# First block of a two-block layer: modulation products shared with TensorE, and moved past other work

## The reference, cut to what matters

```python
ada = c @ w_ada[layer] + b_ada[layer]                    # 1024 -> 6144
shift1, scale1, gate1, shift2, scale2, gate2 = split(ada, 6)
h = rms_norm(x, g_norm1) * (1 + scale1) + shift1
z = h @ w_in                                             # 3524 wide
q, k, ik = rms_norm(zq), rms_norm(zk), rms_norm(zik)     # per head
y_attn = dsa_attention(q, k, zv, ziq, ik, ziw) @ w_up_attn
y_pool = pool_mixer(zp, w_pool_grp, s_pool) @ w_up_pool
mixed = (g_attn * y_attn + g_pool * y_pool) @ w_out
x = x + gate1 * mixed
h2 = rms_norm(x, g_norm2) * (1 + scale2) + shift2
x = x + gate2 * peer_ffn(h2, ...)                        # 16384 experts
```

## Time and profile before

| | |
|---|---|
| median of 3 runs | 1739.95 us (1735.2, 1740.91, 1739.95) |
| profiled execution, own time | 1738.6 us, span 1736.8 us |
| mean granted clock of TensorE | 0.970 |
| PE busy | 1597.0 us (92%) |
| DVE busy | 1170.0 us (67%) |
| POOL busy | 1153.6 us (66%) |
| ACT busy | 867.8 us (50%) |

### The profile page before, as it was taken

How to read it: one execution, slowest core, us unless ns; L and a number is a source line. 1 busy time by engine, 2 the same in 40 slices (tenths; PEclk the granted TensorE clock), 3 DMA queues, 4 the chain that set the end, 5 groups by cost and what they waited for, 6 DMA issues and landing times.

```text
span 1736.8 us, 27719 instructions
## 1 busy us (share of the span) xinstructions
PE 1597.0 (92%) x9959; PEld 1398.7 (81%) x9959; DVE 1170.0 (67%) x1695; ACT 867.8 (50%) x1475; POOL 1153.6 (66%) x468
## 2 busy tenths in 40 slices
PE   1788977999999999999999999899978988899999
PEld 1665536999999999978888888889757756789987
DVE  6564546899937777768888888652995276268760
ACT  1443204555566666645555555559634455354452
POOL 0662005689986666668888888759974821668886
PEclk9899889999999999999999999999989899999999
DMA  7645255455454444445555555546544610445554
GB/s 266 222 150 193 100 218 188 157 181 176 161 184 143 137 143 137 146 141 192 192 194 191 192 193 194 164 159 195 179 136 130 198 61 13 145 146 184 182 183 143
DMA packets 79271, 286.94 MB, mean 165 GB/s; under 512 B 8785, under 2 KB 9297, under 8 KB 79058
## 3 DMA queue, kind: packets, MB, share of 16 engines
q1 hardware_dynamic: 78464, 283.51, 49.1%
q10 hardware_dynamic: 722, 2.27, 0.4%
HBM read 284.70 MB, written 1.05 MB: 165 GB/s over the span
## 4 chain that ended last, share of the span: by engine, by line
PE 77%; DVE 11%; POOL 4%; ACT 3%; issue 3%; DMA 2%; ACTq 0%; SPq 0%; POOLq 0%; DVEq 0%
PE PS L340 22%; PE PS L341 21%; PE PS L342 21%; POOL low L1921 4%; PE PS L338 3%; DVE region L1743 2%; DMA ring<-in_stream 2%; PE PS L719 2%; PE PS L461 1%; PE PS L718 1%; DVE region L1460 1%; PE PS L783 1%; PE PS L551 1%; ACT region L979 1%; DVE region L1747 1%
## 5 line engine op out<-in xcount | busy, mean ns | idle before, releaser
L1921 POOL TENSOR_TENSOR low<-ring,high 128x1024 fp32r<-128x1024 f32 x464 | 1153.4, 2498 | 572.5 <-ACT high L914 572.2
L914 ACT ACTIVATE high<-ring 128x1024 fp32r<-128x1024 f32 x464 | 488.2, 1058 | 438.3 <-PE PS L342 412.8
L340 PE MATMUL PS<-hTh,high 128*128 128x256 f32 (+1 forms) x1728 | 494.1, 286 | 6.1 <-POOL low L1921 4.6
L341 PE MATMUL PS<-hTl,high 128*128 128x256 f32 (+1 forms) x1728 | 489.6, 283 | 0.0
L342 PE MATMUL PS<-hTh,low 128*128 128x256 f32 (+1 forms) x1728 | 489.0, 283 | 0.0
L340 PE MATMUL PS<-high,hTh 128*128 128x512 f32 x960 | 381.7, 398 | 18.2 <-POOL low L1921 14.1
L341 PE MATMUL PS<-low,hTh 128*128 128x512 f32 x960 | 377.8, 394 | 0.0
L342 PE MATMUL PS<-high,hTl 128*128 128x512 f32 x960 | 377.3, 393 | 0.0
L340 PEld LDWEIGHTS PS<-hTh,high 128*128 128x128 f32 (+1 forms) x1728 | 322.9, 187 | 7.9 <-POOL low L1921 3.9
L1691 DVE TENSOR_TENSOR hTl<-region,hTh 128x256 fp32r<-128x256 f32 x128 | 289.2, 2260 | 58.7 <-ACT hTh L1146 58.7
L341 PEld LDWEIGHTS PS<-hTl,high 128*128 128x128 f32 (+1 forms) x1728 | 323.0, 187 | 0.1
(11 more groups left out here) (282 smaller groups left out, 1634.2 us busy)
## 6 DMA issues: line engine op xcount, KB each, us to landing
ring<-in_stream SPq DMA_DIRECT2D x536, 512.0 KB, 3.3
X<-in_x SPq DMA_DIRECT2D x1, 1024.0 KB, 4.9
region<-in_band ACTq DMA_DIRECT2D x1, 1024.0 KB
result<-X SPq DMA_DIRECT2D x4, 256.0 KB, 2.0
region<-in_skeys ACTq DMA_DIRECT2D x1, 512.0 KB
region<-in_consts ACTq DMA_DIRECT2D x1, 352.0 KB, 3.6
region<-in_wpool ACTq DMA_DIRECT2D x1, 256.0 KB
cols<-in_cols SPq DMA_DIRECT2D x1, 228.0 KB, 5.0
```

Of the source, the lines that this page charges most:

```text
L340: pe.matmul(out_, sh, mh, start=start, stop=False, **kw)
L341: pe.matmul(out_, sh, ml, start=False, stop=False, **kw)
L914: act.activation(high[:, b % RING, :], ring[:, b % RING, :], ACT.Copy).then_inc(rounded[b % RING], 1)
L1921: pool.tensor_tensor(low[:, b % RING, :], ring[:, b % RING, :], high[:, b % RING, :].bitcast(F32), ALU.subtract).then_inc(left[b % RING], 1)
```

## The change

- Start: each of `ada` 0 to 3 is shared out. TensorE takes quarters 0 and 2 (`ADA_ON_PE`): two float32 matmuls for each, whose stationary operand is one column of `c` and whose moving operand is 512 columns of weights; the result is one row of PSUM. ACT copies that row to SBUF, and TensorE's sums take it in by one more matmul per 128 outputs (a stationary operand of one partition), 16 passes in place of 8. DVE does quarters 1 and 3. TensorE does the products of block j before the sums of block j-1.
- The decay constants move on DVE from behind `ada(0)` to behind the attention, and their exponential on ACT to just before the attention.
- Queries and keys: per token tile, two `tensor_tensor` of 128 columns (broadcast inputs) in place of four `tensor_scalar` of 64; the copy of 256 columns goes, and TensorE transposes those two chunks from `Z`.
- `ada(9)` and `ada(4)` on DVE move into the attention, one quarter behind each of the eight units. The stream's order becomes `up_pool`/`ada8`, `ada9`, `ada4`, `up_attn`.
- The sums of `ada` 6 to 9 on TensorE move behind the transposes of the mixed sum; the wait for `ada_kept` moves from before `out0` to behind it.
- The mixed sum: `up_attn` finishes its last two quarters bank by bank, into banks 4 to 7, and signals each bank. DVE mixes a bank as it comes; the transposes of the first four chunks need three banks mixed, the others all four.

```diff
-    for name in [f"in{i}" for i in range(Z1B)] + ["up_pool", "up_attn", "ada4", "out0", "out1", "pq0", "pq1"]:
+    for name in [f"in{i}" for i in range(Z1B)] + ["up_pool", "ada9", "ada4", "up_attn", "out0", "out1", "pq0", "pq1"]:
...
+        ADA_ON_PE = (0, 2)
...
             def transposes(tag, src, ready, n_ready, chunk=None, first_half=None):
-                pe.wait_ge(sem(ready), n_ready)
+                pe.wait_ge(sem(ready), first_half or n_ready)
                 for c in range(KC):
+                    if first_half and c == KC // 2:
+                        pe.wait_ge(sem(ready), n_ready)
...
-                        last = pe.matmul(PS[:, 7, 4 * j + q:4 * j + q + 1], src[:, q * P:(q + 1) * P],
-                                         ones[:, 0:1], start=True, stop=True)
+                        dst = PS[:, 7, 4 * j + q:4 * j + q + 1]
+                        last = pe.matmul(dst, src[:, q * P:(q + 1) * P], ones[:, 0:1], start=True, stop=(j >= 4))
+                        if j < 4:
+                            last = pe.matmul(dst, ada_row[0:1, j, q * P:(q + 1) * P], ones[0:1, 0:1],
+                                             start=False, stop=True)
...
+            def ada_products(j):
+                for q in ADA_ON_PE:
+                    wait_loaded(pe, f"ada{j}", q)
+                    for c in range(2):
+                        last = pe.matmul(PS[0:1, 5 + j % 2, :], col("cT", 2 * q + c), slot(f"ada{j}", q)[:, c, :],
+                                         start=(q == ADA_ON_PE[0] and c == 0), stop=(q == ADA_ON_PE[-1] and c == 1))
+                    if q != ADA_ON_PE[-1]:
+                        free_slot(f"ada{j}", q, last)
+                free_slot(f"ada{j}", ADA_ON_PE[-1], last)
...
-            for j in range(4):
-                wait_used(pe, f"ada{j}")
-                ada(j)
+            for j in range(5):
+                if j < 4:
+                    if j >= 2:
+                        pe.wait_ge(sem("ada_row_kept"), j - 1)
+                    ada_products(j)
+                if j:
+                    wait_used(pe, f"ada{j - 1}")
+                    pe.wait_ge(sem("ada_row_kept"), j)
+                    ada(j - 1)
...
-            for j in (6, 7, 8):
+            attention("a1")
+
+            pe.wait_ge(sem("attn1_kept"), 2)
+            token_major("up_attn", OT1, lambda t, o: 4 + 2 * t + o, per=1, inner=D, bank_done="up_done")
+            transposes("m1", M1, "m1_ready", 4, first_half=3)
+            for j in (6, 7, 8, 9):
                 wait_used(pe, f"ada{j}")
                 ada(j)
-            attention("a1")
-
-            pe.wait_ge(sem("attn1_kept"), 2)
-            token_major("up_attn", OT1, lambda t, o: 2 * t + o, per=1, inner=D)
-            wait_used(pe, "ada9")
-            ada(9)
-            transposes("m1", M1, "m1_ready", 1)
             pe.wait_ge(sem("turned_kept"), kept_by("m1", KC))
-            pe.wait_ge(sem("ada_kept"), 2)
...
             token_major("out0", MT1, lambda t, o: 4 + 2 * t)
+            pe.wait_ge(sem("ada_kept"), 2)
...
+            for j in range(4):
+                wait_used(act, f"ada{j}", ADA_ON_PE[-1])
+                act.activation(ada_row[0:1, j, :], PS[0:1, 5 + j % 2, :], ACT.Copy).then_inc(sem("ada_row_kept"), 1)
...
+                    if tag == "a1" and u < n:
+                        ada((9, 4)[u // QUARTERS], [u % QUARTERS])
...
-                for dup in range(2):
-                    dve.tensor_scalar(N1[:, t, 512 + dup * HD:576 + dup * HD], Z[:, t, K1:K1 + HD],
-                                      st1[:, 2, r0 + 8:r0 + 9], None, ALU.mult)
-                    dve.tensor_scalar(N1[:, t, 896 + dup * HD:960 + dup * HD], Z[:, t, IK1:IK1 + HD],
-                                      st1[:, 2, r0 + 9:r0 + 10], None, ALU.mult)
-                link(dve.tensor_copy(N1[:, t, 640:896], Z[:, t, IQ1:IQ1 + 256]))
+                for w, (o, src) in enumerate(((512, K1), (896, IK1))):
+                    ins = dve.tensor_tensor(N1[:, t, o:o + P].rearrange("p (e d) -> p e d", e=2),
+                                            bc(Z[:, t, src:src + HD], 1, 2),
+                                            st1[:, 2, r0 + 8 + w:r0 + 9 + w].unsqueeze(1).broadcast_to([P, 2, HD]),
+                                            ALU.mult)
+                link(ins)
...
             for t in range(T):
                 for half in range(2):
+                    if t and half:
+                        wait_used(dve, "up_attn")
+                    else:
+                        dve.wait_ge(sem("up_done"), 2 * t + half + 1)
                     o = half * NB
-                    res = PS[:, 2 * t + half, :]
+                    res = PS[:, 4 + 2 * t + half, :]
                     link(dve.tensor_tensor(res, res, Z[:, t, G1 + o:G1 + o + NB], ALU.mult))
-                    link(dve.tensor_tensor(M1[:, t, o:o + NB], res, y_pool[:, t, o:o + NB], ALU.add))
-            dve.memset(m8[:, :], 0.0).then_inc(sem("m1_ready"), 1)
+                    dve.tensor_tensor(M1[:, t, o:o + NB], res, y_pool[:, t, o:o + NB],
+                                      ALU.add).then_inc(sem("m1_ready"), 1)
```

More of the change, by code:

```diff
@@ L81 @@
 NCOL = _at
-PAIRED = {"in1": "ada6", "in6": "ada7", "up_pool": "ada8", "up_attn": "ada9", "out0": "ada5", "out1": "ada10",
+PAIRED = {"in1": "ada6", "in6": "ada7", "up_pool": "ada8", "out0": "ada5", "out1": "ada10",
           "pq1": "ada11"}
@@ L215, in build_program @@
         late_acc = take(ADA_B - 4, NB)
+        ada_row = late_acc[0:1, 0:4, :]
         y_pool = XN1
@@ L612, in _ @@
                 z1(i)
-            transposes("qk1", N1, "qk1_normed", 1)
+            transposes("qk1", N1, "qk1_normed", 1, lambda t, c: (Z if c in (5, 6) else N1)[:, t, c * P:(c + 1) * P])
             z1(3)
@@ L1074, in _ @@
             keep_turned("m1", MT1)
+            act.wait_ge(sem("ada_summed"), 8)
+            act.activation(adaT[:, 24:40], PS[:, 7, 24:40], ACT.Copy).then_inc(sem("ada_copied"), 1)
             for i in range(2):
@@ L1445, in bc, with ada @@
                 return v.broadcast_to(shape)
-            def ada(j):
+            def ada(j, part=range(QUARTERS)):
                 if j in (2, 3):
                     dve.wait_ge(sem("ada_summed"), j - 1)
-                for q in range(QUARTERS):
+                qs = [q for q in range(QUARTERS) if j >= 4 or q not in ADA_ON_PE]
+                for n, q in enumerate(qs):
+                    if q not in part:
+                        continue
                     wait_loaded(dve, f"ada{j}", q)
                     w = slot(f"ada{j}", q)
-                    if q:
-                        wait_used(dve, f"ada{j}", q - 1)
+                    if n:
+                        wait_used(dve, f"ada{j}", qs[n - 1])
                     for c in range(2):
-                        if q == c == 0:
-                            ins = dve.tensor_scalar(ada_acc(j), w[:, 0, :], col("cT", 0), None, ALU.mult)
+                        if n == c == 0:
+                            ins = dve.tensor_scalar(ada_acc(j), w[:, 0, :], col("cT", 2 * q), None, ALU.mult)
                         else:
@@ L1473, in _ @@
             ada(0)
-            dve.wait_ge(sem("lam_exp"), 1)
-            link(dve.tensor_scalar(s[3], s[1], 2.0, None, ALU.add))
-            link(dve.reciprocal(s[4], s[3]))
-            link(dve.tensor_tensor(s[5], s[1], s[4], ALU.mult))
-            link(dve.tensor_tensor(s[6], s[5], s[5], ALU.mult))
-            link(dve.tensor_scalar(s[7], s[6], 1.0 / 15, 1.0 / 13, ALU.mult, ALU.add))
-            for k in (11, 9, 7, 5, 3, 1):
-                link(dve.tensor_tensor(s[7], s[7], s[6], ALU.mult))
-                link(dve.tensor_scalar(s[7], s[7], 1.0 / k, None, ALU.add))
-            link(dve.tensor_tensor(s[7], s[7], s[5], ALU.mult))
-            link(dve.tensor_scalar(s[7], s[7], 8.0, None, ALU.mult))
-            link(dve.tensor_scalar(s[2], s[2], 0.0, 4.0, ALU.max, ALU.mult))
-            link(dve.tensor_tensor(s[7], s[7], s[2], ALU.add))
-            dve.tensor_scalar(s[6], s[7], -2.0, None, ALU.mult).then_inc(sem("decay_ready"), 1)
             for j in range(1, 4):
@@ L1568, in _ @@
             dve.wait_ge(sem("ada_copied"), 1)
-            link(dve.tensor_tensor(adaT[:, 24:36], adaT[:, 24:36], bada[:, 24:36], ALU.add))
-            dve.wait_ge(sem("ada_summed"), 8)
-            dve.tensor_tensor(adaT[:, 36:40], PS[:, 7, 36:40], bada[:, 36:40], ALU.add).then_inc(sem("ada_kept"), 1)
+            dve.tensor_tensor(adaT[:, 24:40], adaT[:, 24:40], bada[:, 24:40], ALU.add).then_inc(sem("ada_kept"), 1)
             dve.wait_ge(sem("ada_kept"), 2)
```

27 lines of the change are left out of this document (18 added, 9 removed).

## The result

The changed kernel took 1718.58 us (median of 1725.23, 1718.58 and 1715.51), against 1739.95. The ratio is 0.9893, 95% interval [0.9857, 0.993].

The account below looks back on a forecast made before the run. PE, busy 92% of the span, was taken as the bound, with time gained only where it waits or runs slowly. Terms -3.8 - 0.9 + 3.0 - 6.7 + 2.2 = -6.2 us gave 1733.7 us, range 1727 to 1746.

Parts of the forecast that it names:

- From `up_attn` to `out0`: Stretch from `up_attn` to `out0`: 24.9 us in place of 31.6, 6.7 us gained.
- low start of `up_attn`: At `up_attn`: products start at the low clock, adding 2.5 us to 14.4 us.
- Attention: In the attention: sums ahead go, 3.75 us earlier, but DVE's quarters lengthen it; 3.0 us lost, bounds 0 and 5.
- Start: Modulation blocks 0 to 3: DVE leaves the path, last sums end at 38.8 against 42.6 us, 3.8 us gained.
- rival 2: At the start: one-column products never lift the clock, PE becomes the bound; 1745.5 us, chance 0.16.
- rival 1: At the start: clock flips, up in products and down in sums, so nothing is gained; 1738 us, chance 0.20.
- the ring: At the start: loop of filling and using weight slots, 6.1 to 6.5 us per block, level with PE's 6.2.
- Queries and keys: Query and key normalisation: new `tensor_tensor` still wait for POOL; 0.9 us gained, bounds 0.5 and 8.
- the bound of 8 us for no waits: At queries and keys: upper bound if DVE never waits for POOL, chain ending at 91 us.
- `out0` starts low: At `out0`: the sums ahead make the clock fall, so it starts low; 2.2 us lost, bounds 0 and 3.
- theory A: Experiments' theory: gain lies where the change works, mostly between `up_attn` and `out0`; what lies behind is carried one for one.
- B: Experiments' other theory: a good part of the gain is how low-clock stretches fall, in the block and behind it.

Follow-up runs that it names:

- e1: The changed kernel run again with no edit: median 1718.39 us, ratio 0.9888 to the kernel before.
- e4: The changed kernel with the keys scaled by ScalarE, VectorE left only the two 512-column `tensor_tensor`: median 1713.96 us, ratio 0.9864.
- e7: The changed kernel with all four banks mixed at once after the last product, not bank by bank: median 1729.65 us, ratio 0.9952.
- e9: The changed kernel with the 32 sums of `ada` 6 to 9 behind `out1` instead of ahead of `out0`: median 1718.39 us, ratio 0.9895.
- e10: The changed kernel with keys scaled on ScalarE and the sums of `ada` 6 to 9 behind `out1`: median 1706.19 us, ratio 0.984.
- e3: The changed kernel with the start undone (modulation blocks 0 to 3 and decay constants as before): median 1726.93 us, ratio 0.9944.
- e6: The changed kernel with TensorE's sums of `ada` 6 to 8 ahead of the attention again: median 1726.33 us, ratio 0.9942.
- e11: The same kernel as e9, run again: median 1718.37 us, ratio 0.9898.
- e12: The same kernel as e10, run again: median 1709.86 us, ratio 0.9837.
- e5: The changed kernel with the quarters of `ada(9)` and `ada(4)` behind the attention again, stream order kept new: median 1734.11 us, ratio 0.9998.
- e2: The kernel before with only the start's part (products on TensorE, decay constants behind the attention): median 1735.49 us, ratio 0.9989.
- e8: The kernel before, unchanged, run for a second trace: 1736.95 us.

## Why the prediction was off

**The step that failed is "From `up_attn` to `out0`".** It gave 24.9 us where both traces measured 19.9, so 11.7 gained instead of 6.7. These 5.0 us are the largest part of the 9.1 between the sum of the forecast (-6.2) and the traced difference (-15.3). What is wrong are sizes; the order of events is as told. Its parts:

- The 2.5 us for a low start of `up_attn`. It ran high in the changed kernel's trace and in e1, e4, e7, e9 and e10 (14.0 us each). PE did come out of the attention low, as forecast (0.50 from 193 to 197 us in the changed kernel), but the clock rose just as `up_attn` began. In e3, e6, e11 and e12 it started low and took 16.6 to 16.7 us (e5, behind its wait, 15.5). e9 and e11 are one kernel, e10 and e12 another. So both levels occur with the same code, and a term that was there in full in four of eleven traces stood in the sum at its full price.
- The 32 sums at 0.16 us a pass, 5.1 us. That price is of the 24 sums of before, which drove into a low clock. At the high clock they took 3.63, 0.113 a pass, and `out0` started 3.5 us behind their start: 1.6 us.
- The rest, 0.9 us: `up_attn` at 13.8 rather than 14.4 up to the transposes, and 0.4 us put in for semaphores that the trace doesn't show.

**Attention: +3.0, measured +1.2.** The earlier start was 3.75 in the forecast and 3.2 measured; the lengthening 6.8, and 4.4 measured (22.5 to 26.9). Late units are 3.05 to 3.2 us apart and not 3.43: a quarter takes 1.44 us of DVE from its start to the next instruction's (184.00 to 185.44), not 1.65. I had added the link of a chain that waits to one that is always late. (Its last addition is off by 0.2 too: 195.2 + 5.9 + 1.65 + 1 is 203.75, not 203.5.) That PE ran low in it was right up to 186 us only; then it stood at 1.00 up to 193.

**Start: -3.8, measured -2.5.** Half right. Behind the first one-column products the clock was high, so rival 2 falls, and the sums cost 0.155 us a pass, as told. But rival 1, up in the products and down again, does not fall. Eleven traces have this start, and in eight of them (e1, e2, e4, e6, e7, e9, e10, e11) the granted clock fell back to 0.50 between 19 and 24 us; eight passes of products with such a stretch in them took 5.0 to 5.3 us, and 3.7 at the high clock. In e7 it fell twice, in e9 three times. PE's timeline of e9:

```profile
25.18 5.29 PE L492 MATMUL PS<-ring,cols 128*1 128x512 f32 x8
...
32.88 5.29 PE L492 MATMUL PS<-ring,cols 128*1 128x512 f32 x8
```

The transposes of the normed x start between 37.4 (e5) and 43.1 us (e9). The three traces without such a fall have them at 38.7 in the mean (40.05, 37.4, 38.6), the eight others at 40.5: the forecast's 38.8 is the undisturbed case, and rival 1 takes nearly half of the gain back. The changed kernel's first trace had no fall and still lost time to the ring, which I took as level with PE's loop and hidden in it: PE waits 0.35 to 1.8 us for it before four of six quarters, and the three blocks behind the first take 7.0 us each (13.9 to 34.9) instead of 6.6. (The forecast's text counts four turns of the ring up to block 3; its 33.2 us hold three.)

**Queries and keys: -0.9, measured -0.8.** Right, with its reason. I named the bound of 8 us for no waits; e4 is that case, obtained with another engine.

**`out0` starts low: +2.2, measured +0.6 to the second norm.** It did start low, in the changed kernel and e1, e3, e4, e5 and e7, all with 32 sums ahead of it; with 8 or none (e6, e9 to e12) it started high in all five traces. That the sums do it here is thus shown. They are not the only way: in e2 and e8 it started low too, behind 12 us of idle and the transposes. Of the size, 1.7 us is the price of the 3.4 us at 0.50. The base was wrong: the other trace of before has a low start too.

**The whole.** The terms make -15.3 us between the traced executions. The medians are 19 to 21 apart. Behind the second norm the two kernels differ by 1.6 us, all seven traces of e1 to e7 lie within 1459.8 to 1465.5 us there, and nothing in the code differs; theory A holds for the bulk. The other 4 to 6 us are not attributed to a place. (Of the traced 15.3, the 0.7 at `up_pool` come from e8's trace alone: 58.4 us from the queries' transposes to there, against 57.5, 57.3 and 57.4.) Both traced executions of the changed kernel (1725.23 and 1719.64) lie above its medians, 4 us in the mean, and e3, e6 and e7 fit that: at the second norm they are 4.1, 4.8 and 8.2 us behind the changed kernel's traces, in the medians 8.5, 7.9 and 11.3. So the traces of the changed kernel look like unlucky ones. That the low stretches decide those 4 us, as B has it, fits the first of them (granted clock 0.969, against 0.972 in the two faster executions beside it) but is argued, not shown: between 165 and 285 us both have less low-clock time than e3, e6 and e7 (31 and 27 us against 34 to 37). B doesn't make the gain. My range took the terms' errors one at a time, and held no room for three of them lying on the same side.

## What to carry to other kernels

Where one engine is busy over 90% and waits for another at a single place, empty that place of everything first: here bank by bank mixing, and the modulation moved in front, made an earlier start worth more than the 2 us that it brought alone. An edit that reorders a consumer of a ring must reorder the stream too (e5: 14.2 us of waiting). And price a step at the clock level measured for it, with each of the two levels as a case with a chance, since the same code shows both.

## What the hardware showed that I had not expected

- Matmuls with a moving operand of one column, 32 in a row at 0.113 us each, were followed by a granted clock of 0.50 in six traces of six ahead of `out0`, though PE was busy all the time; matmuls with a stationary operand of one column and 512 moving columns were followed by the high level (5.34 us for the first eight passes, 1.88 for the next four).
- The Trainium skill (TensorE: Matmul & The Clock Gate, "Part 4: PE-mode transpose") says that transposes don't count as busy for the clock. The trace of before does not bear it out. There PE had been idle for 11.8 us and then did transposes alone from 227.43 on the earlier trace rows; the granted clock rose to 1.00 at 230.2, before any other matmul:

```profile
227.40:230.10 2.70, 2.67 (x13) 2.67 (x14) 0.00 (x0) 1.32 (x4) 0.00 (x0) 0.50 0.00 0
230.30:230.90 0.60, 0.44 (x4) 0.20 (x2) 0.60 (x2) 0.00 (x0) 0.00 (x0) 1.00 0.00 0
```

It need not rise so soon: in e8 and e2 it stayed at 0.50 through 3.7 us of transposes. That it holds 1.00 over a gap says less: before, it did so for the first 4.3 us of plain idle (215.7 to 220.0), so the 3.9 us of transposes and waits between two stretches at 1.00 in e10 decide nothing.

- ACT scales 64 columns in 0.25 us beside a POOL instruction that makes the same work on DVE take 2.4 us; once POOL has finished, DVE too takes 0.25.
- The spread between executions of one kernel (1698.75 to 1715.81 in e10) goes with the mean granted clock: 0.977 at the fastest, 0.966 at the slowest.
